# Two transformer layers on one core: the indexer's key group with x stationary, later transfers for the mixed groups, and latents turned in blocks

## The chip, the cores and the metric

The kernel runs on one core of a Trainium2 chip. The metric is the device time of one execution in microseconds, the median of several runs. The core has five engines that run side by side and wait for each other only through semaphores: TensorE (PE in the rows, with its weight loads as PEld), VectorE (DVE), ScalarE (ACT), GpSimd (POOL) and SyncE (SP), which here issues transfers. SP and ACT each have a queue that issues transfers in program order (SPq, ACTq).

## The reference, cut to what matters

Two layers follow one another on x, 256 positions by 2048 channels, all fp32. The parts that the change touches:

```python
# first layer, h = rmsnorm(x)
z = h @ w_in                       # 5200 columns
k_idx = z[..., 5120:5184]          # indexer keys, 64 columns
w_idx = z[..., 5184:5200] * 16 ** -0.5 * 64 ** -0.5
rel = relu(q_idx . k_idx);  iscore = sum over heads of rel * w_idx   # picks 64 keys a query
# second layer, xn = rmsnorm(h)
proj = xn @ w_in_2
c_q, c_kv = proj[..., 3072:3584], proj[..., 3584:3840]   # latents, 512 and 256 columns
qh = rmsnorm(c_q, q_norm) @ w_uq;  kv = rmsnorm(c_kv, kv_norm) @ w_ukv
mixed = g_a * (y_a @ w_branch_a) + g_b * (y_b @ w_branch_b)
h = h + mixed @ w_out
```

## The kernel before, in words

**Products.** All large products are made of three: each operand is split into a high part (rounded to fp32r) and a low part (the rest, also fp32r), and high times high, high times low and low times high are added up. The weights stream in from HBM in chunks, most of them 2 tiles of 128 rows by 512 columns (512 KB). There are 844 chunks in 102 groups; a group is one block of columns of one weight matrix and fills one pair of PSUM banks (`acc`, one bank for each half of 128 positions; two pairs take turns). For a chunk of 512 columns TensorE makes 12 products (`columns`, L754 to L756): a 128 by 128 piece of x is stationary, 512 weight columns move.

**A chunk's way.** A ring of four slots holds the chunks. SP loads one (`load`, L510), ACT copies its high part (`split`, L1081), DVE subtracts for the low part (L1447), TensorE uses it. SP may load chunk c once DVE has split chunk c-4; ACT may split chunk c once TensorE has done chunk c-4; TensorE may start chunk c once DVE has split it.

**Steps.** Everything else is a step: `plan` puts it at a chunk number n by hand (`put(n, ...)`), and each engine runs the steps that are its own. TensorE runs the steps of n after chunk n. ACT and DVE run them after they have split chunk n+3. SP runs them after it has issued the load of chunk n+7 (`at.get(chunk.now - RING - LEAD - 1)`). Nothing is reordered: a step that waits holds back all that stands behind it on its engine or queue.

**Indexer keys** (group 2, chunks 16 and 17, each 8 tiles by 80 columns). `kw_columns` has the weights stationary (128 by 80) and x moving (256 columns): 48 products, L798 to L800, into one bank, with the result turned over (80 rows by 256 positions). ACT copies it to `stage` (`copy_kw`), TensorE turns it back (`turn_kw`, two turns, L745), and DVE scales it into `widx` and `kdup` (`evac_kw`). TensorE then turns `kdup` into the keys (`turn_ki`, step 21), ACT copies them (step 22). The first use is `rel` at step 25.

**Latents.** c_q is group 41 (chunks 378 to 385), c_kv group 42 (386 to 393). ACT evacuates to `stage`, TensorE turns them in the step after (`turn_lat`, 8 and 4 turns, L745), and ACT and DVE split them from the banks one step later (`split_lat`). `w_uq_2` (chunk 418) and `w_ukv_2` (chunk 448) use them.

**Mixed groups.** The gated sum has four blocks of 512 columns, n = 0 to 3. For each there are 4 chunks of `w_branch_a_2` and 4 of `w_branch_b_2`, chunks 516+8n to 523+8n; then comes the output projection `w_out_2` from chunk 548. With b = 524+8n, the chunk number right after the block's last chunk: DVE's step b is `mix_b` (two products with the gate from PSUM, L1699, two sums, L1702, two turns in blocks of 32 by 32, L1601). The blocks are then moved across partitions by 16 transfers of 32 KB each (`move_block`, L382). For n below 3 SP issues four of them in each of the steps b to b+3, and ACT and DVE split the result in step b+7 (`split_mix`, L1239 and L1595). For n = 3 SP issues ten in step b, ACT six in step b+1, and the split is step b+3. The transfers wait for `mix_blocks`, which `mix_b` sets at its end. In the first group of `w_out_2` TensorE waits before its chunk 0 for the split of blocks 0 and 1, before chunks 4 and 5 for the two halves of block 2, and before chunks 6 and 7 for those of block 3:

```python
elif name == "w_out_2" and col == 0:
    need = {k: (mix_low, 8 - n) for k, n in ((0, 4), (4, 3), (5, 2), (6, 1), (7, 0))}
```

Of the kernel before, what the change touches and what calls it, by code (L numbers as in the profile page):

```python
# [54 lines left out]
def plan():  # L55
# [73 lines left out]
    put(b, "copy_kw", len(groups) - 1); put(b + 1, "turn_kw", len(groups) - 1); put(b + 1, "evac_kw")  # L129
    put(b + 3, "turn_ki"); put(b + 4, "copy_ki")  # L130
# [36 lines left out]
    put(b + 1, "turn_lat", "ckv", len(groups) - 1)  # L167
    put(b + 2, "split_lat", "ckv"); put(b + 2, "lat_rstd", "ckv"); put(b + 1, "rope", "kr", len(groups) - 1)
# [65 lines left out]
def two_layer_kernel(nc, a, out):  # L234
# [6 lines left out]
    with ctx:  # L241
# [107 lines left out]
        kw_turned, kw_scaled = sem("kw_turned"), sem("kw_scaled")  # L349
# [15 lines left out]
        p_blocks, p_moved = sem("p_blocks"), sem("p_moved")  # L365
        mix_blocks, mix_moved = sem("mix_blocks"), sem("mix_moved")
# [23 lines left out]

        def shares(part):

            return range(SP_SHARE) if part is None else range(4 * part, 4 * part + 4)
# [6 lines left out]
        def move_mix(queue, n, which):  # L400

            queue.wait_ge(mix_blocks, n + 1)
            move_blocks_of(queue, which, flat_half, flat_stage[1], mix_moved)

# [78 lines left out]
        def _(sp):  # L483
# [12 lines left out]
            def load(name, col, width, c):  # L496
# [233 lines left out]
        def _(pe):  # L730
            chunk, group, splits, copies = Count(), Count(), Count(), Count()
            rels, atts, pvs, lats = Count(), Count(), [0], []
# [58 lines left out]
            def kw_columns(c, g):  # L791
# [60 lines left out]
            def turn_kw(g):  # L852

                wait_bank(0)
                pe.wait_ge(acc_taken[g % 2], 2 * (g // 2 + 1))
                for t in range(NT):
                    last = turn(0, t * KW, stage[0:KW, g % 2, 0, t * P:(t + 1) * P], KW)
                last.then_inc(kw_turned, 1)
                free[0] = (kw_scaled, NT)

            def turn_ki():
                wait_bank(0)
# [115 lines left out]
            def on_turn_stage(g, banks, wait):  # L978
                pe.wait_ge(*wait)
                for b in banks:  # L980
                    wait_bank(b)
                    four(b, lambda cc, t: stage[:, g % 2, t, (2 * b + cc) * P:(2 * b + cc + 1) * P], split_full, 1)
                    splits.now += 1
                    free[b] = (split_lo, splits.now)

            def on_turn_lat(kind, g):
                on_turn_stage(g, range(2 if kind == "cq" else 1), (acc_taken[g % 2], 2 * (g // 2 + 1)))
                lats.append(splits.now)

# [9 lines left out]
            def on_turn_kn(k, g):  # L999
# [6 lines left out]
            mine = {"turn_kw": turn_kw, "turn_ki": turn_ki, "turn_copy": turn_copy, "rel": on_rel, "scores": on_scores,  # L1006
                    "pv": on_pv, "pool_d": on_pool_d, "pool_y": on_pool_y,
                    "turn_lat": on_turn_lat, 
# [26 lines left out]
            while g < len(groups):  # L1035
# [31 lines left out]
        def _(act):  # L1067
# [64 lines left out]

            def on_copy_kw(g):
                finished(g)
                stage_free(g)
                for t in range(NT):
                    act.activation(stage[0:KW, g % 2, 0, t * P:(t + 1) * P], acc[g % 2][0][0:KW, t * P:(t + 1) * P],
                                   ACT.Copy).then_inc(acc_taken[g % 2], 1)
# [92 lines left out]
            def on_split_lat(kind):  # L1231
                o, gain = (cqT, G_CQ) if kind == "cq" else (ckvT, G_CKV)
                for b in range(2 if kind == "cq" else 1):
                    high([o[:, 0, 2 * b], o[:, 0, 2 * b + 1]], b, gain + 2 * b)
# [47 lines left out]
            mine = {"evac": on_evac, "copy_kw": on_copy_kw, "copy_ki": on_copy_ki, "copy2": on_copy2, "copy_k": on_copy_k, "relu": on_relu, "exp": on_exp,  # L1282
# [143 lines left out]
        def _(dve):  # L1426
# [26 lines left out]
            def on_evac_kw():  # L1453

                dve.wait_ge(kw_turned, 1)
                dve.wait_ge(rstd_ready, 1)
                for t in range(NT):
                    r, key = rstd[:, t:t + 1], T[0][:, t * KW:t * KW + IDX_DIM]
                    dve.tensor_scalar(widx[:, t], T[0][:, t * KW + IDX_DIM:(t + 1) * KW], r, 2.0 ** -5, ALU.mult, ALU.mult)
                    dve.tensor_scalar(kdup[:, t, 0:64], key, r, None, ALU.mult)  # L1460
                    dve.tensor_scalar(kdup[:, t, 64:128], key, r, None, ALU.mult).then_inc(kw_scaled, 1)
# [123 lines left out]

            def on_split_lat(kind):
                o, gain = (cqT, G_CQ) if kind == "cq" else (ckvT, G_CKV)
                for b in range(2 if kind == "cq" else 1):
                    low([o[:, 1, 2 * b], o[:, 1, 2 * b + 1]], [o[:, 0, 2 * b], o[:, 0, 2 * b + 1]], b, gain + 2 * b)
# [105 lines left out]
            def on_mix_b(n, g):  # L1695
# [8 lines left out]
                for t in range(NT):  # L1704
# [5 lines left out]
                    "split_pool": on_split_pool, "split_lat": on_split_lat, "split_mix": on_split_mix, "res": on_res,  # L1710
# [208 lines left out]
```

## Time and profile before

| | |
|---|---|
| median of 3 runs | 2373.63 us (2372.42, 2373.67, 2373.63) |
| the profiled execution's own time | 2370.55 us |
| its span, first to last instruction | 2368.8 us |
| mean granted TensorE clock | 0.999 of full speed |
| TensorE busy | 2354.6 us, 99% of the span |
| weight loads busy (beside the products) | 1949.5 us, 82% |
| VectorE, ScalarE, GpSimd busy | 59%, 50%, 3% |
| DMA engines busy with q1 packets | 69.5% |

The page gives busy time by engine, the groups of instructions by line, and the chain of work that ended last. A product's record lasts longer than its place in the stream: the products overlap, so what one costs is the distance from its start to the next one's. In the timeline, a line with "x8" is eight instructions in a row, shown with the first one's start and their whole length; a bracket at the end is idle time before it and what ended it.

### The profile page before, as it was taken

To read this page: it belongs to the slowest core of one execution; us is meant where nothing else is said; L and a number is where in the kernel's file an instruction comes from. 1 tells how busy PE (TensorE), PEld (TensorE's weight loads), DVE (VectorE), ACT (ScalarE), POOL (GpSimd) and SP (SyncE) were. 2 spreads that over 40 slices of the span, in tenths; PEclk is the share of its full clock that TensorE was granted. 3 is DMA by queue.
4 is the path that set the end of the run, shared out by engine and by line. 5 is a ranking of instruction groups with operands and counts; after the bars stand their busy time and mean duration, and the time that the engine had idled before them with its cause. 6 is when DMAs were issued, how large, how long until landed. Compare 5 with 4: busy or idle time off the path is not lost.

```text
span 2368.8 us, 29833 instructions
## 1 busy us (share of the span) xinstructions
PE 2354.6 (99%) x10552; PEld 1949.5 (82%) x10552; DVE 1399.9 (59%) x1586; ACT 1186.1 (50%) x1465; POOL 59.4 (3%) x94
## 2 busy tenths in 40 slices
PE   9999999999999999999999999999999999999998
PEld 7788888888888888888888888878888888888887
DVE  6786465676776765555565554766555555554544
ACT  6445455666666544445455554544544444444443
POOL 0000000000000000001130000000000000000000
PEclk9999999999999999999999999999999999999999
DMA  9776477788787766666787666666777777767664
GB/s 304 195 216 192 153 225 209 215 227 220 202 226 219 206 219 201 201 203 195 210 215 209 181 175 197 200 202 208 230 204 200 209 203 204 209 199 220 194 195 153
DMA packets 490442, 488.24 MB, mean 206 GB/s; under 512 B 248304, under 2 KB 275568, under 8 KB 490224
## 3 DMA queue, kind: packets, MB, share of 16 engines
q1 hardware_dynamic: 467888, 482.85, 69.5%
q10 hardware_dynamic: 22464, 4.20, 0.9%
q8 instruction: 56, 0.92, 0.2%
q14 instruction: 34, 0.28, 0.0%
HBM read 448.12 MB, written 2.10 MB: 190 GB/s over the span
## 4 chain that ended last, share of the span: by engine, by line
PE 96%; SPq 1%; DVE 1%; DMA 1%; ACT 0%; issue 0%; POOLq 0%; POOL 0%; DVEq 0%; ACTq 0%
PE acc L754 31%; PE acc L756 31%; PE acc L755 31%; SPq L382 1%; PE pair_banks L923 1%; DMA w_raw<-in_w_branch_a 1%; DVE w_lo L1447 0%; PE bank L942 0%; ACT w_hi L1081 0%; DMA w_raw<-in_w_in 0%; PE pair_banks L972 0%; PE pair_banks L895 0%; PE acc L780 0%; PE acc L784 0%; PE acc L787 0%
## 5 line engine op out<-in xcount | busy, mean ns | idle before, releaser
L1447 DVE TENSOR_TENSOR w_lo<-w_raw,w_hi 128x1024 fp32r<-128x1024 f32 (+1 forms) x842 | 1024.1, 1220 | 934.8 <-ACT w_hi L1081 933.2
L1081 ACT ACTIVATE w_hi<-w_raw 128x1024 fp32r<-128x1024 f32 (+1 forms) x842 | 886.0, 1055 | 1077.1 <-PE acc L756 980.9
L754 PE MATMUL acc<-w_hi,xT 128*128 128x512 f32 (+1 forms) x2208 | 861.4, 390 | 0.0
L756 PE MATMUL acc<-w_hi,xT 128*128 128x512 f32 (+1 forms) x2208 | 856.8, 388 | 0.0
L755 PE MATMUL acc<-w_lo,xT 128*128 128x512 f32 (+1 forms) x2208 | 856.7, 388 | 0.0
L754 PEld LDWEIGHTS acc<-w_hi,xT 128*128 128x128 f32 x2208 | 414.5, 188 | 87.1 <-issue 2.7
L756 PEld LDWEIGHTS acc<-w_hi,xT 128*128 128x128 f32 x2208 | 414.5, 188 | 85.4
L755 PEld LDWEIGHTS acc<-w_lo,xT 128*128 128x128 f32 x2208 | 414.6, 188 | 83.8
L754 PE MATMUL acc<-w_hi,f_hi 128*128 128x512 f32 x688 | 267.6, 389 | 0.0
L755 PE MATMUL acc<-w_lo,f_hi 128*128 128x512 f32 x688 | 267.6, 389 | 0.0
L756 PE MATMUL acc<-w_hi,f_lo 128*128 128x512 f32 x688 | 267.6, 389 | 0.0
L755 PEld LDWEIGHTS acc<-w_lo,f_hi 128*128 128x128 f32 x688 | 129.2, 188 | 27.0
L754 PEld LDWEIGHTS acc<-w_hi,f_hi 128*128 128x128 f32 x688 | 129.2, 188 | 26.7
L756 PEld LDWEIGHTS acc<-w_hi,f_lo 128*128 128x128 f32 x688 | 129.2, 188 | 26.7
L754 PE MATMUL acc<-w_hi,y_hi 128*128 128x512 f32 x256 | 100.0, 391 | 0.0
L756 PE MATMUL acc<-w_hi,y_lo 128*128 128x512 f32 x256 | 99.6, 389 | 0.0
L755 PE MATMUL acc<-w_lo,y_hi 128*128 128x512 f32 x256 | 99.6, 389 | 0.0
L755 PEld LDWEIGHTS acc<-w_lo,y_hi 128*128 128x128 f32 x256 | 48.1, 188 | 10.0
L754 PEld LDWEIGHTS acc<-w_hi,y_hi 128*128 128x128 f32 x256 | 48.1, 188 | 9.9
L756 PEld LDWEIGHTS acc<-w_hi,y_lo 128*128 128x128 f32 x256 | 48.1, 188 | 9.9
L754 PE MATMUL acc<-w_hi,m_hl 128*128 128x512 f32 x128 | 49.9, 390 | 3.8 <-DVE w_lo L1447 3.8
L755 PE MATMUL acc<-w_lo,m_hl 128*128 128x512 f32 x128 | 49.8, 389 | 0.0
(211 smaller groups left out, 1217.4 us busy)
## 6 DMA issues: line engine op xcount, KB each, us to landing
w_raw<-in_w_up SPq DMA_DIRECT2D x264, 512.0 KB, 4.2
w_raw<-in_w_in SPq DMA_DIRECT2D x198, 512.0 KB, 4.3
w_raw<-in_w_down SPq DMA_DIRECT2D x176, 512.0 KB, 4.5
w_raw<-in_w_gate SPq DMA_DIRECT2D x88, 512.0 KB, 3.7
w_raw<-in_w_out SPq DMA_DIRECT2D x64, 512.0 KB, 4.3
w_raw<-in_w_branch_a SPq DMA_DIRECT2D x16, 512.0 KB, 4.5
w_raw<-in_w_branch_b SPq DMA_DIRECT2D x16, 512.0 KB, 4.4
halves<-stage SPq DMA_DIRECT2D x234, 32.0 KB, 2.7
```

The lines of the kernel that those rows point to most:

```text
L382: return queue.dma_start(dst, src)
L754: pe.matmul(o, l, w_hi[:, slot, k, 0:width], start=start, stop=False)
L755: pe.matmul(o, l, w_lo[:, slot, k, 0:width], start=False, stop=False)
L756: last = pe.matmul(o, m, w_hi[:, slot, k, 0:width], start=False, stop=stop)
L923: last = pe.matmul(pair_banks[:, j, blk * P:blk * P + nk], q[:, blk * P:(blk + 1) * P], k[:, 0:nk], start=alone or blk == 0, stop=alone, s ...
L1081: act.activation(in_slot(w_hi, slot, width), in_slot(w_raw, slot, width), ACT.Copy).then_inc(w_split_hi, 1)
L1447: dve.tensor_tensor(in_slot(w_lo, slot, width), in_slot(w_raw, slot, width), in_slot(w_hi, slot, width).bitcast(F32), ALU.subtract).then_i ...
```

## The change

It has three parts. First, in the group of indexer keys x is stationary (128 by 128) and the 80 weight columns move: 96 products into two banks; `copy_kw` and `turn_kw` are gone, `evac_kw` reads the accumulators one step earlier, and `turn_ki` and `copy_ki` come one step earlier. Second, the transfers of the mixed groups start two steps later: for n below 3 six, six and four in the steps b+2 to b+4, with the split still at b+7; for n = 3 ten from SP and six from ACT, both in step b+2, and the split at b+5. Third, the latents are turned by DVE in blocks of 32 by 32 (`lat_blocks`) and moved across partitions by 16 transfers from SP (four in each of four steps, `move_lat`), and split from SBUF at b+13, in place of the turns on TensorE.

```diff
@@ plan
-    put(b, "copy_kw", len(groups) - 1); put(b + 1, "turn_kw", len(groups) - 1); put(b + 1, "evac_kw")
-    put(b + 3, "turn_ki"); put(b + 4, "copy_ki")
+    put(b, "evac_kw", len(groups) - 1)
+    put(b + 2, "turn_ki", len(groups) - 1); put(b + 3, "copy_ki")
...
-    put(b + 1, "turn_lat", "cq", len(groups) - 1)
-    put(b + 2, "split_lat", "cq"); put(b + 2, "lat_rstd", "cq")
+    put(b + 1, "lat_blocks", "cq", len(groups) - 1)
+    for part in range(4):
+        put(b + 2 + part, "move_lat", "cq", part)
+    put(b + 13, "split_lat", "cq"); put(b + 2, "lat_rstd", "cq")
...
-        for part in range(4) if n < 3 else (None,):
-            put(b + (part or 0), "move_mix", n, part)
+        for part in range(3) if n < 3 else (None,):
+            put(b + 2 + (part or 0), "move_mix", n, part)
         if n == 3:
-            put(b + 1, "move_mix_rest", n)
-        put(b + (7 if n < 3 else 3), "split_mix", n)
+            put(b + 2, "move_mix_rest", n)
+        put(b + (7 if n < 3 else 5), "split_mix", n)
@@ two_layer_kernel
+        def thirds(part):
+
+            return range(SP_SHARE) if part is None else range(6 * part, min(6 * part + 6, 16))
+
+        def latents(kind):
+
+            if kind == "cq":
+                return 0, 4, over_y[0][:], over_y[4][:], cqT, G_CQ
+            return 1, 2, over_y[1][:, 0:CW], over_y[1][:, CW:2 * CW], ckvT, G_CKV
@@ sync
-                            move_mix(sp, args[0], shares(args[1]))
+                            move_mix(sp, args[0], thirds(args[1]))
+            def move_lat(kind, b):
+
+                k, _, blocks_, moved, _, _ = latents(kind)
+                sp.wait_ge(lat_blocks, k + 1)
+                for a_ in range(4):
+                    move_block(sp, moved, blocks_, b, a_).then_inc(lat_moved[k], 16)
@@ tensor, kw_columns
-                    h, l, o = hi[:, k * KW:(k + 1) * KW], lo[:, k * KW:(k + 1) * KW], acc[g][0][0:KW, 0:S]
-                    pe.matmul(o, h, xT_hi[:, kt], start=kt == 0, stop=False)
-                    pe.matmul(o, h, xT_lo[:, kt], start=False, stop=False)
-                    last = pe.matmul(o, l, xT_hi[:, kt], start=False, stop=kt == KT - 1)
+                    h, l = hi[:, k * KW:(k + 1) * KW], lo[:, k * KW:(k + 1) * KW]
+                    for t in range(NT):
+                        o, rows = acc[g][t][:, 0:KW], slice(t * P, (t + 1) * P)
+                        pe.matmul(o, xT_hi[:, kt, rows], h, start=kt == 0, stop=False)
+                        pe.matmul(o, xT_hi[:, kt, rows], l, start=False, stop=False)
+                        last = pe.matmul(o, xT_lo[:, kt, rows], h, start=False, stop=kt == KT - 1)
...
-                    need = {0: (split_lo, lats[0])}
+                    need = {0: (lat_low, 1)}
...
-                    need = {0: (split_lo, lats[1])}
+                    need = {0: (lat_low, 2)}
@@ scalar
             def on_split_lat(kind):
+                k, nq, _, _, o, gain = latents(kind)
+                act.wait_ge(lat_moved[k], 256)
+                for q in range(nq):
+                    last = act.activation(o[:, 0, q].rearrange("p (n k) -> p n k", n=2 * 4), turned_latent(kind, q), ACT.Copy,
+                                          scale=cols[:, gain + q:gain + q + 1])
+                last.then_inc(lat_high, 1)
@@ vector
-            def on_evac_kw():
+            def on_evac_kw(g):
+                finished(g)
...
-                    r, key = rstd[:, t:t + 1], T[0][:, t * KW:t * KW + IDX_DIM]
+                    r, key = rstd[:, t:t + 1], acc[g % 2][t][:, 0:IDX_DIM]
...
+            def on_lat_blocks(kind, g):
+                _, nq, blocks_, _, _, _ = latents(kind)
+                dve.wait_ge(acc_taken[g % 2], 2 * (g // 2 + 1))
+                for t in range(NT):
+                    last = dve.transpose(blocks_.rearrange("p (t b q k) -> p t q b k", t=NT, b=4, q=nq)[:, t],
+                                         stage[:, g % 2, t, 0:nq * P])
+                last.then_inc(lat_blocks, 1)
```

DVE's `split_lat` changes in the same way as ScalarE's: one subtraction for each 128 columns from the moved blocks.

## Rows read from the trace of the kernel before

**Rows 1.** The page: busy times, shares of the last chain, one kind of DMA issue.

```profile
PE 2354.6 (99%) x10552; PEld 1949.5 (82%) x10552; DVE 1399.9 (59%) x1586; ACT 1186.1 (50%) x1465; POOL 59.4 (3%) x94
...
PE 96%; SPq 1%; DVE 1%; DMA 1%; ACT 0%; issue 0%; POOLq 0%; POOL 0%; DVEq 0%; ACTq 0%
...
w_raw<-in_w_in SPq DMA_DIRECT2D x198, 512.0 KB, 4.3
```

**Rows 2.** Waits of TensorE: who waited for whom, us in total, times, longest.

```profile
PE acc L754 <- DVE w_lo L1447: 3.8, 2, 2.5
```

**Rows 3.** Groups by line and shape: busy us, mean ns of one, idle before.

```profile
L1447 DVE TENSOR_TENSOR w_lo<-w_raw,w_hi 128x1024 fp32r<-128x1024 f32 x832 | 1015.8, 1224 | 925.6 <-ACT w_hi L1081 924.0
L1081 ACT ACTIVATE w_hi<-w_raw 128x1024 fp32r<-128x1024 f32 x832 | 878.8, 1059 | 1070.9 <-PE acc L756 974.8 <-DMA w_raw<-in_w_in 36.1 <-DMA w_raw<-in_w_out 20.1
...
L754 PEld LDWEIGHTS acc<-w_hi,xT 128*128 128x128 f32 x2208 | 414.5, 188 | 87.1 <-issue 2.7
...
L798 PEld LDWEIGHTS acc<-xT,w_hi 128*80 128x80 f32 x16 | 2.4, 148 | 0.0
```

**Rows 4.** Timeline around the group of indexer keys: start us, us, engine, line.

```profile
49.27 0.39 PE L755 MATMUL acc<-w_lo,xT 128*128 128x512 f32 x1
...
50.17 0.39 PE L756 MATMUL acc<-w_hi,xT 128*128 128x512 f32 x1
...
50.40 0.28 PE L798 MATMUL acc<-xT,w_hi 128*80 128x256 f32 x1
50.40 0.15 PEld L799 LDWEIGHTS acc<-xT,w_hi 128*80 128x80 f32 x1
...
55.87 0.28 PE L800 MATMUL acc<-xT,w_lo 128*80 128x256 f32 x1
```

**Rows 5.** The same view: the first scores, on plain fp32 operands.

```profile
143.17 1.47 PE L923 MATMUL pair_banks<-k1T,q1T 128*128 128x128 f32 x8
...
144.71 0.40 PE L755 MATMUL acc<-w_lo,xT 128*128 128x512 f32 x1
```

**Rows 6.** The same view: turns on TensorE, of keys and of the first latents.

```profile
61.47 0.30 PE L745 MATMUL bank<-ident,stage 80*128 80x80 f32 x2
...
61.88 0.40 PE L755 MATMUL acc<-w_lo,xT 128*128 128x512 f32 x1
...
1092.84 1.04 PE L745 MATMUL bank<-ident,stage 128*128 128x128 f32 x8
...
1093.86 0.31 PE L755 MATMUL acc<-w_lo,xT 128*128 128x320 f32 x1
```

**Rows 7.** The same view: the sync queue's transfers in the mixing stage.

```profile
1545.54 3.49 SPq L382 DMA_DIRECT2D halves<-stage  x4
...
1562.80 6.38 SPq L382 DMA_DIRECT2D halves<-stage  x10
```

**Rows 8.** The same view: VectorE at the first mixed group and the last.

```profile
1491.55 1.30 DVE L1601 STREAM_TRANSPOSE stage<-stage 128x512 f32<-128x512 f32 x2
...
1558.82 1.28 DVE L1699 TENSOR_TENSOR gate<-acc,gate 128x512 f32<-128x512 f32 x2
...
1561.46 1.30 DVE L1601 STREAM_TRANSPOSE stage<-stage 128x512 f32<-128x512 f32 x2
1562.69 1.18 DVE L1447 TENSOR_TENSOR w_lo<-w_raw,w_hi 128x1024 fp32r<-128x1024 f32 x1
...
1570.91 1.43 DVE L1595 TENSOR_TENSOR m_hl<-halves,m_hl 128x256 fp32r<-128x256 f32 x4 [0.42 <-ACT m_hl L1239]
```

**Rows 9.** The same view: ScalarE's queue and copies at the last mixed group.

```profile
1562.80 4.13 ACTq L382 DMA_DIRECT2D halves<-stage  x6
...
1570.46 1.34 ACT L1239 ACTIVATE m_hl<-halves 128x256 fp32r<-128x256 f32 x4 [1.42 <-DMA halves<-stage]
```

**Rows 10.** The same view: TensorE's idle starts in the output projection.

```profile
1564.02 0.47 PE L754 MATMUL acc<-w_hi,m_hl 128*128 128x512 f32 x1 [1.29 <-DVE w_lo L1447]
...
1569.50 0.47 PE L754 MATMUL acc<-w_hi,m_hl 128*128 128x512 f32 x1 [2.48 <-DVE w_lo L1447]
```

More of the change, by code:

```diff
@@ L162, in plan @@
     put(b, "evac", "stage", len(groups) - 1); put(b + 1, "lat_square", "cq", len(groups) - 1)
-    put(b + 1, "turn_lat", "cq", len(groups) - 1)
-    put(b + 2, "split_lat", "cq"); put(b + 2, "lat_rstd", "cq")
+    put(b + 1, "lat_blocks", "cq", len(groups) - 1)
+    for part in range(4):
+        put(b + 2 + part, "move_lat", "cq", part)
+    put(b + 13, "split_lat", "cq"); put(b + 2, "lat_rstd", "cq")
     b = group("w_in_2", 3584, 320, whole, "x")
     put(b, "evac", "ckv", len(groups) - 1); put(b + 1, "lat_square", "ckv", len(groups) - 1)
-    put(b + 1, "turn_lat", "ckv", len(groups) - 1)
-    put(b + 2, "split_lat", "ckv"); put(b + 2, "lat_rstd", "ckv"); put(b + 1, "rope", "kr", len(groups) - 1)
+    put(b + 1, "lat_blocks", "ckv", len(groups) - 1)
+    for part in range(4):
+        put(b + 2 + part, "move_lat", "ckv", part)
+    put(b + 13, "split_lat", "ckv"); put(b + 2, "lat_rstd", "ckv"); put(b + 1, "rope", "kr", len(groups) - 1)
     put(b + 4, "turn_kr"); put(b + 5, "copy_kr")
@@ L365, in two_layer_kernel @@
         p_blocks, p_moved = sem("p_blocks"), sem("p_moved")
+        lat_blocks, lat_high, lat_low = sem("lat_blocks"), sem("lat_high"), sem("lat_low")
+        lat_moved = [sem("cq_moved"), sem("ckv_moved")]
         mix_blocks, mix_moved = sem("mix_blocks"), sem("mix_moved")
@@ L403, in move_mix, with turned_latent @@
             move_blocks_of(queue, which, flat_half, flat_stage[1], mix_moved)
+        def latents(kind):
+            if kind == "cq":
+                return 0, 4, over_y[0][:], over_y[4][:], cqT, G_CQ
+            return 1, 2, over_y[1][:, 0:CW], over_y[1][:, CW:2 * CW], ckvT, G_CKV
+        def turned_latent(kind, q):
+            _, nq, _, moved, _, _ = latents(kind)
+            return moved.rearrange("p (n q k) -> p n q k", n=2 * 4, q=nq)[:, :, q]
         def p_source(which, pair):
@@ L849, in stream, with turn_ki @@
                 group.now += 1
-            def turn_kw(g):
+            def turn_ki(g):
                 wait_bank(0)
                 pe.wait_ge(acc_taken[g % 2], 2 * (g // 2 + 1))
[L856 to L862, printed above, removed]
                 turn(0, 0, kdup[:, 0])
@@ L976, in on_pool_y @@
                     free[2 + w] = (split_lo, splits.now)
[L978 to L988, printed above, removed]
             def on_turn_kr():
@@ L1004, in on_turn_kn @@
                 free[0] = (copy_done, copies.now)
-            mine = {"turn_kw": turn_kw, "turn_ki": turn_ki, "turn_copy": turn_copy, "rel": on_rel, "scores": on_scores,
+            mine = {"turn_ki": turn_ki, "turn_copy": turn_copy, "rel": on_rel, "scores": on_scores,
                     "pv": on_pv, "pool_d": on_pool_d, "pool_y": on_pool_y,
-                    "turn_lat": on_turn_lat,
                     "turn_kr": on_turn_kr, "turn_kn": on_turn_kn}
@@ L1131, in copied @@
                 act.activation(out_, T[bank][:, 0:width], ACT.Copy, scale=scale).then_inc(copy_done, 1)
[L1133 to L1138, printed above, removed]
             def on_copy_ki():
@@ L1231, in on_split_lat @@
             def on_split_lat(kind):
-                o, gain = (cqT, G_CQ) if kind == "cq" else (ckvT, G_CKV)
-                for b in range(2 if kind == "cq" else 1):
-                    high([o[:, 0, 2 * b], o[:, 0, 2 * b + 1]], b, gain + 2 * b)
+                k, nq, _, _, o, gain = latents(kind)
[4 more added lines that the diff above has]
+                last.then_inc(lat_high, 1)
             def on_split_mix(n):
@@ L1451, in finished @@
                 dve.wait_ge(w_used, first[g] + len(groups[g][3]))
-            def on_evac_kw():
-                dve.wait_ge(kw_turned, 1)
+            def on_evac_kw(g):
+                finished(g)
                 dve.wait_ge(rstd_ready, 1)
                 for t in range(NT):
-                    r, key = rstd[:, t:t + 1], T[0][:, t * KW:t * KW + IDX_DIM]
-                    dve.tensor_scalar(widx[:, t], T[0][:, t * KW + IDX_DIM:(t + 1) * KW], r, 2.0 ** -5, ALU.mult, ALU.mult)
+                    r, key = rstd[:, t:t + 1], acc[g % 2][t][:, 0:IDX_DIM]
+                    dve.tensor_scalar(widx[:, t], acc[g % 2][t][:, IDX_DIM:KW], r, 2.0 ** -5, ALU.mult, ALU.mult)
                     dve.tensor_scalar(kdup[:, t, 0:64], key, r, None, ALU.mult)
-                    dve.tensor_scalar(kdup[:, t, 64:128], key, r, None, ALU.mult).then_inc(kw_scaled, 1)
+                    dve.tensor_scalar(kdup[:, t, 64:128], key, r, None, ALU.mult).then_inc(acc_taken[g % 2], 1)
             def on_headsq(name, g):
@@ L1584, in on_split_pool @@
                     low([y_lo[:, k], y_lo[:, k + 1]], [y_hi[:, k], y_hi[:, k + 1]], 2 + w, G_POOL + k)
-            def on_split_lat(kind):
-                o, gain = (cqT, G_CQ) if kind == "cq" else (ckvT, G_CKV)
-                for b in range(2 if kind == "cq" else 1):
-                    low([o[:, 1, 2 * b], o[:, 1, 2 * b + 1]], [o[:, 0, 2 * b], o[:, 0, 2 * b + 1]], b, gain + 2 * b)
+            def on_lat_blocks(kind, g):
[5 more added lines that the diff above has]
+                last.then_inc(lat_blocks, 1)
+            def on_split_lat(kind):
+                k, nq, _, _, o, gain = latents(kind)
+                dve.wait_ge(lat_high, k + 1)
+                for q in range(nq):
+                    lo_, hi_ = (o[:, n, q].rearrange("p (n k) -> p n k", n=2 * 4) for n in (1, 0))
+                    last = dve.scalar_tensor_tensor(lo_, turned_latent(kind, q), cols[:, gain + q:gain + q + 1],
+                                                    hi_.bitcast(F32), ALU.mult, ALU.subtract)
+                last.then_inc(lat_low, 1)
             def on_split_mix(n):
```

9 lines of the change are left out of this document (5 added, 4 removed).

## The prediction

> **What bounds the kernel now.** The page comes first: TensorE is busy 99% of the span, and 96% of the chain that ended last is its products [rows 1]. A microsecond taken from TensorE's stream, or added to it, is a microsecond of the kernel; work on the other engines counts only where it makes TensorE wait. The waits of TensorE say where it does so in mid-kernel: twice, for the low parts of weights [rows 2]. The timeline puts both into the output projection of layer two, before chunks 552 and 553 [rows 10]. The idle shown there is 1.29 and 2.48 us; the real loss is more, as each record before it reaches 0.39 - 0.23 = 0.16 us past its place and the first product after it is 0.08 longer: 1.53 and 2.72, together 4.25 us. Five products of 512 columns take 50.40 - 49.27 = 1.13 us, 0.227 each [rows 4], so a chunk of twelve is 2.72 us; 512 columns at the 2.4 GHz level are 0.213 of the 0.227, and 13 ns are left over per change of weights.
>
> **Part 1, the indexer's keys.** Before: 48 products from 50.40 to 55.87 [rows 4], 47 distances of 0.116 us, so 5.6 us in all; 256 columns are 107 ns of it, 10 ns are left over. After: 96 products of 80 columns, 33 ns of streaming each. So short a product no longer hides its weight load. A load of 128 columns is on record for 188 ns, one of 80 for 148 [rows 3]: 40 ns for 48 columns, 0.83 ns a column, hence 107 ns of loading for 128 columns, the rest being a fixed part. A load starts with the product before it (both at 50.40 [rows 4]) and must be through before its own product starts, so the distance is at least 107 ns, and with the 10 or so left over 0.116: 96 x 0.116 = 11.1 us, a term of +5.5. That x's high part is stationary twice in a row saves nothing by the profile, since L754 and L755 share theirs in the same way and every product has its own load. Bounds: if streaming set the distance (33 + 13 ns), 96 x 0.047 = 4.5 us, -1.1. If so narrow a product ran at the rate of plain fp32, it would be slower: the first scores are 8 instructions, 4 of 128 and 4 of 256 columns, and TensorE is free for L754 0.23 before L755, at 144.48, so 1536 columns in 1.31 us [rows 5], two clocks a column; a plain product is two such instructions, four clocks. Then 0.133 + 0.013 = 0.147 each, 14.1 us, +8.5. I take 11.1, because the slope of the loads is of this very operand type and the other two ends need something that no row shows.
>
> The Trainium skill has a rule that speaks for the low end: by "TensorE: Matmul & The Clock Gate", section on Fast Weight Load, weights of 128 columns that are not fp32 load about twice as fast. By it the part would cost 96 x (53 + 13) ns = 6.4 us, +0.8. The trace disagrees so far: 128 columns, at 188 ns, lie on the slope from the 80-column load and not below it [rows 3].
>
> The turns that go: two of 80 columns, from 61.47 to 61.65 (L755 at 61.88 less 0.23), 0.2 us at most; eight of the first latents, from 1092.84 to 1093.71 (1093.86 less the 0.15 of a 320-column product), 0.87 us, 0.109 each [rows 6]; four more for the second, 0.44. Together -1.5. The scaling on DVE one step earlier costs nothing on the path: it waits for chunk 17, done before it can split chunk 21, and its result is wanted by TensorE two chunks on and by the first use at step 25. ScalarE loses two small copies.
>
> **Part 2, latents in blocks.** DVE gets four block turns (0.65 us each at 512 columns [rows 8], so at most 2.6), SP gets 32 transfers. One costs SP 0.638 us (ten in 6.38 [rows 7]); four and a load of some 0.6 are 3.2 us per chunk against 2.72, so SP falls behind by about 2 us in four chunks, twice. That is covered: SP may load chunk c when chunk c-4 is split, and that split begins when chunk c-8 is done, so 7 chunks less the 2.3 us of the split, 16.7 us, before TensorE needs c; landing (4.3 from issue [rows 1]), high part and low part want 6.6 of them. The split at b+13 has its transfers landed long before, and the first user is chunk 418, eleven after the last split. I take 0; with the cover gone it would be up to 2.
>
> **Part 3, the mixed groups.** This part decides the sign. Let E be the end of DVE's two turns for block n; E is 1491.55 + 1.30 = 1492.85 for n = 0 and 1562.76 for n = 3 [rows 8], so blocks follow at 23.3 us, where eight chunks are 21.8: engines fall behind by 1.5 us a block, and this lag is what shows up as the idle before chunk 552. With the change, from E: two low parts (1.23 each, the line's mean [rows 3]) E + 2.4; load of b+9 0.6, E + 3.0; six transfers 3.84, load, six, load, four (16 x 0.638 and two loads at 0.64 in all), last issued E + 14.5; landed 1.3 later (1569.18 to the copy at 1570.46 [rows 7, 9]), E + 15.8; ScalarE, which reached this step earlier and waits, four copies 1.3, then its next high part 1.06 [rows 3], low part 1.23, and 3.94 of mixing and turning (1558.82 to 1562.76): the next E is at + 23.4. That is no better than before, though transfers no longer wait for DVE; SP still has to issue 16 and ScalarE now stands at the split. Before, though, SP also paused in some transfers (four in 3.49 rather than 2.55 [rows 7]); if pauses recur, up to 2 us come on top. So the last E comes 0.3 to 2.3 later, I take 1.1.
>
> For n = 3 the end is what counts. TensorE wants the first half of block 3 before chunk 554. Before: chunk 552 starts at E + 1.3, 553 at E + 6.7 (held up because ScalarE was busy with its six transfers, 4.13 us [rows 9], before it could split 553), 554 at E + 9.5; block 3 was split by then (1570.91 + 0.7 = E + 8.9 [rows 8]). After: ScalarE splits 553 first, so 553 starts at E + 4.0 and 554 could at E + 6.7. But SP's step 550 stands behind the load of chunk 557, that behind the low part of 553, E + 2.4; load 0.6, ten transfers 6.4, landing 1.3, first copies and low parts 1.2: E + 11.9. A wait of 5.2 us before chunk 554 takes the place of the 2.72 before 553: + 2.4. With the later E, **+3.5**. Bounds: even with everything landed at once, the split at step 553 stands behind the split of chunk 556, which wants chunk 552 done: 1.06 + 1.23 + 0.7 = 3.0 after chunk 553 starts, 0.3 past its 2.72; so at best 4.25 - 0.3 = 3.9 us are gained. At worst 2.3 + 2.4 and a pause in the ten transfers of 1: +5.7.
>
> **Sum.** 5.5 - 1.5 + 3.5 = +7.5 us. On the profiled execution's own 2370.55 that is 2378.1; this one was 3.1 below the median of 2373.63, so the median should be 2381.1, 0.32% up. A measurement can tell some 0.2% from no change, 4.7 us.
>
> **Rivals.**
> A. The forecast, new wait before chunk 554 and products bound by loads, with its own spread of 2378 to 2384: 0.57.
> B. Not slower: the later transfers do what they could do. The place is chunks 552 to 554; the price is -3.9 for +3.5. It decides if the split of block 3 is through within 3 us of chunk 553's start, that is, if SP's ten transfers land before E + 7 or so. Then 5.5 - 1.5 - 3.9 = +0.1, 2373.7. For it: ScalarE's and SP's transfers no longer stand before the splits of 552 and 553. Against: ten transfers alone are 6.4 us and cannot begin before E + 3. 0.10.
> C. In between: old waits gone, the new one no longer than they were. +4.0, 2377.7. 0.13.
> D. Narrow products bound by something less than a 107 ns load (the fast load, or streaming): -1.1 to +0.8 for 5.5, so with part 3 as forecast +0.9 to +2.8, 2375.5; with B as well -6.5 to -4.6, about 2368. 0.05 and 0.02.
> E. Four clocks a column: +8.5 for 5.5, 2384.1; with the worst of part 3 2386.3. 0.13.
>
> B, C and the first of D lie within 0.2%, the second of D is faster, A and E are slower save for the lower edge of A (0.05). Faster 0.02, within 0.33, slower 0.65. The range leaves out the second of D, the lower half of B, and the top of E: 2373.5 to 2386.
>
> **What would show it.** Part 1: the new products of 80 columns start 0.11 to 0.12 apart and take 11 us from first to last; 0.15 would be E, 0.07 or less D. The 12 turns of latents are gone, with no new idle in front of w_uq_2. Part 3: TensorE's waits name the low part of block 3 (m_hl, L1595 before) as what releases it before chunk 554, for about 5 us; SP's ten transfers start some 3 us after the last turns, not at once; ScalarE waits for a landing before the copies to m_hl in every block. The forecast is wrong if the output projection shows no idle at chunk 554, or if the key group takes less than 8 us.

## The result, and the profile after

The changed kernel takes 2389.93 us (median of 4, 2389.26 to 2391.07), the kernel before in the same session 2373.31 (median of 4): 1.0076 times as long, 95% interval 1.0063 to 1.0088. It is slower by more than was forecast: +16.6 us by the medians for +7.5, and outside the range. The profiled executions are further apart, 2389.74 and 2370.55, because the one of before lay 2.8 us under its median; by the spans it is 2388.0 - 2368.8 = 19.2, and the stages below add up to that.

The page after, beside [rows 1]:

```profile
PE 2369.5 (99%) x10586; PEld 1962.4 (82%) x10586; DVE 1402.2 (59%) x1590; ACT 1185.9 (50%) x1463; POOL 59.1 (2%) x94
...
PE 95%; DMA 1%; DVE 1%; SPq 1%; ACT 0%; issue 0%; ACTq 0%; POOLq 0%; POOL 0%; DVEq 0%
```

TensorE is the bound as before, and is busy for 14.9 us longer with 34 more instructions. Its idle time grew by only some 4. So most of the loss is inside busy time, where no view of waits shows it. The waits of TensorE after, beside [rows 2]:

```profile
PE acc L783 <- DVE m_hl L1614: 4.0, 1, 4.0
PE acc L783 <- DVE w_lo L1454: 3.7, 3, 2.0
...
PE bank L965 <- DMA halves<-over_y: 1.0, 1, 1.0
```

The first is the wait that was forecast (the low part of block 3, before chunk 554), the second is three waits for low parts of weights, the third is new in the middle of layer two.

To place the 19.2 us, I took from each trace the time at which the last product before a chunk ends, and subtracted those of before. The differences by stage, in us, for the full change and for the three kernels with one part of it each (described below):

| stage | after | keys alone | mixing alone | latents alone | forecast |
|---|---|---|---|---|---|
| start-up, to chunk 16 | +0.2 | +0.2 | +0.6 | +0.7 | 0 |
| keys and the two chunks behind, 16 to 20 | +11.6 | +11.6 | 0 | 0 | +5.5 |
| the keys' turns, 20 to 34 | -0.2 | -0.2 | 0 | 0 | -0.2 |
| the latents' turns, 378 to 402 | -1.35 | 0 | 0 | -1.35 | -1.3 |
| 402 to 448 | +1.3 | +0.4 | 0 | 0 | 0 |
| mixing, 544 to 555 | +7.6 | -1.5 | +8.0 | +1.7 | +3.5 |
| all, to chunk 844 | +19.1 | +10.5 | +8.6 | +1.1 | +7.5 |

No part of the change touches the start-up, so its +0.2 to +0.7 are differences from one execution to another. Two terms missed, the keys by 6 and the mixing stage by 4. For the keys, TensorE by windows (length, then busy us and instructions of PE, PEld, DVE, ACT, POOL; granted clock; DMA share; GB/s), first the stretch from the first narrow product on:

```profile
50.00:56.00 6.00, 6.00 (x54) 5.88 (x52) 1.66 (x2) 2.21 (x3) 0.00 (x0) 1.00 0.95 285
56.00:64.00 8.00, 8.00 (x44) 8.00 (x43) 2.44 (x3) 1.06 (x1) 0.00 (x0) 0.56 0.77 173
64.00:72.00 8.00, 8.00 (x26) 6.55 (x26) 2.46 (x8) 2.12 (x2) 0.00 (x0) 0.59 0.44 99
```

TensorE is busy for every one of these 22 us, yet the granted clock falls from 1.00 to 0.56. The timeline of the same stretch shows where:

```profile
50.58 0.20 PE L829 MATMUL acc<-w_hi,xT 128*128 128x80 f32 x1
...
56.53 0.28 PE L829 MATMUL acc<-w_hi,xT 128*128 128x80 f32 x1
56.64 0.28 PE L830 MATMUL acc<-w_lo,xT 128*128 128x80 f32 x1
56.75 0.29 PE L831 MATMUL acc<-w_hi,xT 128*128 128x80 f32 x1
56.86 0.39 PE L829 MATMUL acc<-w_hi,xT 128*128 128x80 f32 x1
57.06 0.42 PE L830 MATMUL acc<-w_lo,xT 128*128 128x80 f32 x1
57.27 0.41 PE L831 MATMUL acc<-w_hi,xT 128*128 128x80 f32 x1
...
64.95 0.41 PE L831 MATMUL acc<-w_hi,xT 128*128 128x80 f32 x1
...
69.58 0.63 PE L784 MATMUL acc<-w_lo,xT 128*128 128x512 f32 x1
70.00 0.63 PE L785 MATMUL acc<-w_hi,xT 128*128 128x512 f32 x1
70.43 0.48 PE L783 MATMUL acc<-w_hi,xT 128*128 128x512 f32 x1
...
71.22 0.40 PE L783 MATMUL acc<-w_hi,xT 128*128 128x512 f32 x1
71.45 0.39 PE L784 MATMUL acc<-w_lo,xT 128*128 128x512 f32 x1
```

The narrow products start 0.11 apart, then from 56.86 on 0.21 apart; the first products of 512 columns behind them start 0.43 apart, and from about 70.7 on 0.23 to 0.24. That is the 1.2 GHz level for nearly 14 us, and TensorE was busy without a gap for over 6 us before it. From the first narrow product to the last (64.95) the group takes 14.4 us, where the prediction's sign was 11. The mixing stage after, four timelines in turn (TensorE, the sync queue, ScalarE with its queue, VectorE; a bracket is idle time and its releaser), beside [rows 7 to 10]:

```profile
1554.02 0.47 PE L783 MATMUL acc<-w_hi,y_hi 128*128 128x512 f32 x1 [1.49 <-DVE w_lo L1454]
...
1578.63 0.47 PE L783 MATMUL acc<-w_hi,m_hl 128*128 128x512 f32 x1 [2.03 <-DVE w_lo L1454]
...
1579.52 0.63 PE L783 MATMUL acc<-w_hi,m_hl 128*128 128x512 f32 x1
1579.95 0.63 PE L784 MATMUL acc<-w_lo,m_hl 128*128 128x512 f32 x1
...
1589.95 0.80 PE L783 MATMUL acc<-w_hi,m_hl 128*128 128x512 f32 x1 [4.02 <-DVE m_hl L1614]
1590.54 0.63 PE L784 MATMUL acc<-w_lo,m_hl 128*128 128x512 f32 x1
```

```profile
1516.33 2.50 SPq L387 DMA_DIRECT2D halves<-stage  x4
...
1573.54 6.48 SPq L530 DMA_DIRECT2D w_raw<-in_w_out  x3
1580.06 6.63 SPq L387 DMA_DIRECT2D halves<-stage  x10
1586.73 1.61 SPq L530 DMA_DIRECT2D w_raw<-in_w_out  x3
```

```profile
1521.57 1.34 ACT L1246 ACTIVATE m_hl<-halves 128x256 fp32r<-128x256 f32 x4 [3.24 <-DMA halves<-stage]
...
1577.41 3.88 ACTq L387 DMA_DIRECT2D halves<-stage  x6
1581.39 2.97 ACT L1092 ACTIVATE w_hi<-w_raw 128x1024 fp32r<-128x1024 f32 x3 [7.05 <-issue]
1588.69 1.33 ACT L1246 ACTIVATE m_hl<-halves 128x256 fp32r<-128x256 f32 x4 [4.33 <-DMA halves<-stage]
```

```profile
1503.11 1.30 DVE L1620 STREAM_TRANSPOSE stage<-stage 128x512 f32<-128x512 f32 x2
...
1576.07 1.30 DVE L1620 STREAM_TRANSPOSE stage<-stage 128x512 f32<-128x512 f32 x2
...
1589.13 1.43 DVE L1614 TENSOR_TENSOR m_hl<-halves,m_hl 128x256 fp32r<-128x256 f32 x4 [3.15 <-ACT m_hl L1246]
```

The order is the forecast's. E, the end of the last block's turns, is 1577.37 (the first lines of the sync queue and of ScalarE belong to block 0, whose E is 1504.41). SP's ten transfers start 2.7 later, ScalarE stands 4.33 us for their landing, and TensorE starts chunk 554 at E + 12.6. Two things were not forecast: the wait before chunk 544 (1554.02), and half the clock twice, in chunk 552 (products 0.43 apart) and again from 1590.54 on.

### The profile page after: what moved, and what is told of

It reads as the page before. It is cut to its first block, busy times and chain, and to the rows that moved or that the text cites. A ratio compares the mean times of both kernels' runs of the same rounds, so it can differ in the third digit from the quotient of the medians.

```text
span 2388.0 us, 29932 instructions
## 1 busy us (share of the span) xinstructions
PE 2369.5 (99%) x10586; PEld 1962.4 (82%) x10586; DVE 1402.2 (59%) x1590; ACT 1185.9 (50%) x1463; POOL 59.1 (2%) x94
## 4 chain that ended last, share of the span: by engine, by line
PE 95%; DMA 1%; DVE 1%; SPq 1%; ACT 0%; issue 0%; ACTq 0%; POOLq 0%; POOL 0%; DVEq 0%
PE acc L783 30%; PE acc L785 30%; PE acc L784 30%; SPq L387 1%; PE pair_banks L946 1%; DVE w_lo L1454 1%; DMA halves<-stage 0%; PE bank L965 0%; PE acc L809 0%; PE acc L813 0%; PE acc L816 0%; PE pair_banks L995 0%; ACT w_hi L1092 0%; DMA w_raw<-in_w_branch_a 0%; PE pair_banks L918 0%
## 5 line engine op out<-in xcount | busy, mean ns | idle before, releaser
L783 PE MATMUL acc<-w_hi,m_hl 128*128 128x512 f32 x128 | 51.5, 402 | 6.3 <-DVE m_hl L1614 4.0
L785 PE MATMUL acc<-w_hi,m_hl 128*128 128x512 f32 x128 | 50.9, 398 | 0.0
```

The costliest lines, as they stand in the source:

```text
L783: pe.matmul(o, l, w_hi[:, slot, k, 0:width], start=start, stop=False)
L785: last = pe.matmul(o, m, w_hi[:, slot, k, 0:width], start=False, stop=stop)
```

## The experiments

Each kernel was compared with the kernel before on the same chip. The first four share one session (before: 2371.04, 22 runs), the last four another (before: 2371.66, 33 runs).

**Keys alone.** Only part 1 of the change; mixed groups and latents as before.

```diff
 # kernel after
-    put(b + 1, "lat_blocks", "cq", len(groups) - 1)
...
+    put(b + 1, "turn_lat", "cq", len(groups) - 1)
...
-        for part in range(3) if n < 3 else (None,):
-            put(b + 2 + (part or 0), "move_mix", n, part)
+        for part in range(4) if n < 3 else (None,):
+            put(b + (part or 0), "move_mix", n, part)
...
```

> The kernel before with part 1 alone (keys with x stationary). Theory K, clock: the 96 products start 0.113 us apart (10.9 us, +5.3 over the 5.6 of before), and some us into them TensorE's granted clock falls from full to half, in which loads and products take twice as long (0.213 apart), until some us after the group: 11.5 to 12 us slower in all, 2385. Rival: products bound by their loads alone, the fall of the clock in the changed kernel was chance: 5 us slower, 2378.5, no half clock behind the start of the kernel.

Measured: 2381.10 us (5 runs), ratio 1.0041 (1.0027 to 1.0055), +10.1 by the medians. By stages the key group costs what it costs in the full change, +11.6, as expected with the fall of the clock, and the turns give back 0.2. Before the mixing stage it is 12.0 behind, after it 10.5: of the two stalls of before [rows 10] the first is gone here, although nothing in that stage was edited. So how engines stand to each other when they enter the stage is worth a microsecond or two, and no sum of terms sees that.

**Keys with 240 columns moving.** Part 1 again, with the same loads and the same number of products, but each streams 240 columns. The sums in the 160 extra columns are read by nobody, and those in the first 80 are unchanged.

```diff
 # kernel of part 1 alone, kw_columns
-                hi, lo = in_slot(w_hi, slot, KW), in_slot(w_lo, slot, KW)
+                hi, lo = (ring[:, slot].rearrange("p k n -> p (k n)") for ring in (w_hi, w_lo))
...
-                    h, l = hi[:, k * KW:(k + 1) * KW], lo[:, k * KW:(k + 1) * KW]
+                    h, l = hi[:, k * KW:(k + 3) * KW], lo[:, k * KW:(k + 3) * KW]
...
-                        o, rows = acc[g][t][:, 0:KW], slice(t * P, (t + 1) * P)
+                        o, rows = acc[g][t][:, 0:3 * KW], slice(t * P, (t + 1) * P)
```

> Part 1 alone, but each product streams 240 columns, 80 real ones and the 160 that lie behind them in the slot, whose results nobody reads: same number of loads and products. If loads of 107 ns set the distance and the clock fell because the array had little to stream, the distance stays near 0.115 and the clock stays full: 96 x 0.115 = 11.0, 5.4 us slower than before, 2378.7, so 6 us faster than the narrow products that do a third of the work. If the clock falls for another reason (many loads, short instructions): 2385 as with the narrow ones. If streaming set the distance all along: 240 columns take 0.1 + 0.013, no verdict from the distance, only from the clock.

Measured: 2375.29 us (10 runs), ratio 1.0016 (1.0006 to 1.0025), +4.3 by the medians. Three times the streaming is 5.8 us faster than 80 columns. The windows of the same 16 us, first of keys alone, then with 240 columns, and three of the wide products:

```profile
56.00:72.00 16.00, 16.00 (x68) 14.87 (x68) 4.83 (x11) 3.18 (x3) 0.00 (x0) 0.58 0.59 137
```

```profile
56.00:72.00 16.00, 16.00 (x98) 14.13 (x97) 8.38 (x13) 5.57 (x6) 0.00 (x0) 1.00 0.67 150
```

```profile
58.35 0.28 PE L826 MATMUL acc<-w_lo,xT 128*128 128x240 f32 x1
58.47 0.28 PE L827 MATMUL acc<-w_hi,xT 128*128 128x240 f32 x1
58.58 0.27 PE L825 MATMUL acc<-w_hi,xT 128*128 128x240 f32 x1
```

Busy 16.00 of 16.00 in both, but the clock is 0.58 in one and 1.00 in the other. As long as the clock is full, the products are 0.11 to 0.12 apart whether 80 or 240 columns move (0.112 on average in both traces). This splits the term of the keys. From chunk 16 to 20 it is +5.1 with 240 columns and +11.6 with 80: the distance at the full clock costs 5.1, and the clock 6.5 on top. Idle time did not lower the clock, and with the same loads the wider products kept it. That is what this pair shows; it gives no rule for other widths.

**Latents alone.** Only part 2; the rest as before.

```diff
 # kernel after
-    put(b, "evac_kw", len(groups) - 1)
-    put(b + 2, "turn_ki", len(groups) - 1); put(b + 3, "copy_ki")
+    put(b, "copy_kw", len(groups) - 1); put(b + 1, "turn_kw", len(groups) - 1); put(b + 1, "evac_kw")
+    put(b + 3, "turn_ki"); put(b + 4, "copy_ki")
...
```

> The kernel before with part 2 alone (latents in blocks). Theory: the turns' 1.36 us are gained and nothing is lost: 1.4 us faster, 2372. Rival: the 32 added transfers bring the wait of 1.3 us before the products with P at chunk 442 that the changed kernel shows: 0 to 0.1, 2373.3, that wait in the trace again.

Measured: 2371.00 us (10 runs), ratio 0.9999 (0.9989 to 1.0008): no difference, neither the 1.4 us faster of the theory nor the wait of the rival. Its trace, one execution, shows the gain and a loss. The turns' 1.35 us go at chunks 386 to 402, and no wait comes in their place. In the mixing stage +1.7 come back: the two stalls are much those of before (1.41 and 2.47 idle), but behind the second one the clock drops, which it did not in the trace of before. The windows of the same stretch, latents alone and before:

```profile
1565.00:1578.00 13.00, 10.53 (x40) 8.27 (x39) 8.01 (x10) 7.47 (x10) 0.00 (x0) 0.87 0.66 200
```

```profile
1565.00:1578.00 13.00, 10.52 (x47) 8.39 (x46) 8.20 (x10) 7.48 (x10) 0.00 (x0) 1.00 0.64 198
```

The same 10.5 us busy hold 40 products for 47. So a stall of 2.5 us can be followed by half the clock or not; the traces do not show what decides. It need not be the kernel: of the 55 executions of before in the two sessions, 19 had a mean granted clock of 0.998 and took 2372.4 us on average, the other 36 had 0.999 or more and took 2371.0. The trace of before has 0.999 and no half clock in the stage, so its stages may stand for the faster executions only, and where the 1.35 us went in the median of latents alone stays open.

**Mixing alone.** Only part 3; keys and latents as before.

```diff
 # kernel before
-        for part in range(4) if n < 3 else (None,):
-            put(b + (part or 0), "move_mix", n, part)
+        for part in range(3) if n < 3 else (None,):
+            put(b + 2 + (part or 0), "move_mix", n, part)
         if n == 3:
-            put(b + 1, "move_mix_rest", n)
-        put(b + (7 if n < 3 else 3), "split_mix", n)
+            put(b + 2, "move_mix_rest", n)
+        put(b + (7 if n < 3 else 5), "split_mix", n)
```

> The kernel before with part 3 alone (mixed groups' transfers two steps later). Theory M: the long wait for block 3 before chunk 554 and the half clock after it do not need parts 1 and 2: 7.5 us slower (6 to 8), 2381, with 9 us of idle and 2 to 3 of half clock in the chunks 547 to 556. Rival: the step is right but its size came with the shifted phase of the other parts: 3 to 4 us slower, 2377, no half clock.

Measured: 2378.93 us (6 runs), ratio 1.0030 (1.0017 to 1.0042), +7.9. TensorE waits 5.6 us for the low part of block 3 and 3.6 for low parts of weights, and the stage costs +8.0, as expected with half the clock behind the long wait (granted 0.62 from 1578 to 1585). The turns end at 1493.4 for block 0 and 1566.0 for block 3, 24.2 us a block, against 23.3 before and 23.4 forecast. The loss is the same as in the full change and does not need the other parts. Its halves were then tried one at a time.

**Last block alone (n = 3) and first three alone.** The transfers and the split of block 3 two steps later with blocks 0 to 2 as before, and the other way about.

```diff
 # kernel before, last block alone
-            put(b + (part or 0), "move_mix", n, part)
+            put(b + (part or 0) + (2 if n == 3 else 0), "move_mix", n, part)
         if n == 3:
-            put(b + 1, "move_mix_rest", n)
-        put(b + (7 if n < 3 else 3), "split_mix", n)
+            put(b + 2, "move_mix_rest", n)
+        put(b + (7 if n < 3 else 5), "split_mix", n)
```

```diff
 # kernel of part 3 alone, first three alone
-            put(b + 2 + (part or 0), "move_mix", n, part)
+            put(b + (2 if n < 3 else 0) + (part or 0), "move_mix", n, part)
         if n == 3:
-            put(b + 2, "move_mix_rest", n)
-        put(b + (7 if n < 3 else 5), "split_mix", n)
+            put(b + 1, "move_mix_rest", n)
+        put(b + (7 if n < 3 else 3), "split_mix", n)
```

> The kernel before with only block 3 changed: its ten and six transfers in step b+2 and its split at b+5; blocks 0 to 2 as before. Theory L: the last block's late transfers carry most of part 3. Idle before chunk 554 of 5 to 6 us in place of the 2.7 before 553, then about 2 us of half clock: 4 to 6 us slower, 2376. Rival: the new order of blocks 0 to 2 carries it: under 2 us slower here, 2372.5.

> The kernel before with only blocks 0 to 2 changed (six, six and four transfers in steps b+2 to b+4), block 3 as before. Theory L: the lag of a block is no smaller than before, idle of 1.8 us appears before chunk 547 or 548 and the one before 552 stays: 1.5 to 3 us slower, 2373.5. Rival: this part does what it was for, since transfers no longer wait for DVE: 1.5 us faster, 2369.5.

Measured: last block alone 2375.07 (10 runs), ratio 1.0015 (1.0006 to 1.0025), +3.4; first three alone 2374.80 (10 runs), ratio 1.0011 (1.0002 to 1.0021), +3.1. Together +6.5, against +7.9 for part 3 as a whole, within the intervals. The expectations were 4 to 6 and 1.5 to 3, so by the medians the last block came out too low and the first three just above; in their mixing stages the traces have +4.2 and +4.5. TensorE's start of chunk 554 with the last block alone:

```profile
1574.32 0.80 PE L754 MATMUL acc<-w_hi,m_hl 128*128 128x512 f32 x1 [5.42 <-DVE m_hl L1595]
```

SP's ten transfers start here at 1564.60, 2.7 us after the turns' end at 1561.92. Until chunk 554 this kernel is 3.6 us ahead of before, since both old stalls have shrunk to 0.7 us in all; then it loses 7.8 at one chunk, 5.4 of them the wait and 2.2 the half clock behind it (granted 0.60 from 1574 to 1580). That is rival B and the forecast in one trace: the gain was real, and what replaced it larger. The first three alone show the lag and no wait for block 3:

```profile
1543.30 0.47 PE L780 MATMUL acc<-w_hi,y_hi 128*128 128x512 f32 x1 [1.54 <-DVE w_lo L1474]
...
1567.70 0.47 PE L780 MATMUL acc<-w_hi,m_hl 128*128 128x512 f32 x1 [2.05 <-DVE w_lo L1474]
...
1573.16 0.47 PE L780 MATMUL acc<-w_hi,m_hl 128*128 128x512 f32 x1 [2.48 <-DVE w_lo L1474]
```

A third stall of 1.54 us has joined the two of before. It stands before chunk 544, the first of the last branch group; my expectation put it a few chunks later. Behind the last of the three, of 2.48, the clock is low (granted 0.66 from 1573 to 1578), which makes 1.6 of the stage's 4.5.

**Transfers shared out between the queues.** If SP's issue time is what makes the blocks late, ScalarE should take some of it where it waits anyway. For n below 3, SP issues three and ScalarE one transfer in each of four steps (SP b+1 to b+4, ScalarE b+2 to b+5); for n = 3 eight each, SP at once, ScalarE after the split of chunk 553. So shares and steps change together here, and no run takes them apart.

```diff
 # kernel before
-            put(b + (part or 0), "move_mix", n, part)
-        if n == 3:
-            put(b + 1, "move_mix_rest", n)
+            put(b + (1 + part if n < 3 else 0), "move_mix", n, part)
+            put(b + 2 + (part or 0), "move_mix_rest", n, part)
...
-                            move_mix(sp, args[0], shares(args[1]))
+                            move_mix(sp, args[0], range(8) if args[1] is None else range(4 * args[1], 4 * args[1] + 3))
...
-            def on_move_mix_rest(n):
-                move_mix(act, n, range(SP_SHARE, 16))
+            def on_move_mix_rest(n, part):
+                move_mix(act, n, range(8, 16) if part is None else range(4 * part + 3, 4 * part + 4))
```

> The kernel before with the transfers of the mixed groups shared out anew: for blocks 0 to 2 SP issues three in each of the steps b+1 to b+4 and ACT one in each of b+2 to b+5, split at b+7; for block 3 SP issues eight in step b, ACT eight in step b+2, split at b+3. Theory: SP stays under 2.72 us a chunk (0.6 + 3 x 0.64 = 2.5), so no lag is carried from block to block, E comes 6.3 us after chunk 547's end, and neither 552, 553 nor 554 waits: the 4.25 us of idle go, 4 us faster, 2367. Rival: ScalarE's share delays its splits so that the idle only changes place: within 1 us of before, 2371.

Measured: 2367.51 us (11 runs), ratio 0.9985 (0.9976 to 0.9994): 4.2 us faster than before by the medians, as expected. Blocks follow at 22.8 us, and one wait is left in the stage:

```profile
PE acc L753 <- DVE m_hl L1594: 1.7, 1, 1.7
```

The traced execution, 2369.17, is one of the slowest of the eleven; in its mixing stage it is 4.2 us ahead of before until chunk 554 and, after this wait, 2.25. All 22 executions of this kernel and the next have a mean granted clock of 0.999 or more.

**The same with the latents in blocks.** Part 2 of the change on top.

```diff
 # kernel of latents alone; the mixing stage as in the edit above
         for part in range(4) if n < 3 else (None,):
-            put(b + (part or 0), "move_mix", n, part)
-        if n == 3:
-            put(b + 1, "move_mix_rest", n)
+            put(b + (1 + part if n < 3 else 0), "move_mix", n, part)
+            put(b + 2 + (part or 0), "move_mix_rest", n, part)
...
```

> The same with the latents in blocks besides. Theory: both gains add, 4.2 + 1.4 = 5.6 us faster than before, 2365.4, with no half clock behind the start of the kernel. Rival: what the latents' part gains is lost again later, as when it stood alone: no faster than with the shared transfers alone.

Measured: 2366.63 us (11 runs), ratio 0.9979 (0.9970 to 0.9988), 5.0 faster for 5.6 expected and the lowest median of all. Its page:

```profile
PE 2353.4 (100%) x10540; PEld 1948.8 (82%) x10540; DVE 1401.1 (59%) x1590; ACT 1185.3 (50%) x1465; POOL 60.2 (3%) x94
```

There is no idle left in the mixing stage, and the granted clock is 1.00 from 14 to 2355 us. By stages the latents' turns give -1.35 and the mixing stage -3.95, close to the -4.25 that the two stalls of before were worth. Against the kernel before it with shared transfers it is only 0.9 faster by the medians, within their spread; whether the latents' gain adds up is not shown.

## Why the prediction was wrong

**Part 1: the distance was right, the clock was not.** The step that failed is the one that makes of the keys "96 x 0.116 = 11.1 us, a term of +5.5". The distance measured at the full clock is 0.112 for the 0.116 of the sum; neither streaming (0.047) nor four clocks a column (0.147) sets it. It fits the load of 128 columns, and a least distance for every product is out, since the two turns of 80 columns in before start 0.07 apart (0.30 us for two, each record 0.23 [rows 6]); but no run loads fewer columns under so narrow a product. With the clock held full, 240 columns wide, the term is +5.1. What the sum left out is that these 96 products did not keep the clock. It took the full clock of before for granted in a stretch unlike any in before, and its list of signs to look for did not name it either. 6.5 us, measured with 80 and with 240 columns, is what that cost. It is the largest piece of the miss. The turns of the keys gave 0.2, as forecast.

By the rule on Fast Weight Load of the Trainium skill ("TensorE: Matmul & The Clock Gate") the estimate for the distance was 0.066; the trace says 0.112. So the low end of the term, and with it rival D, is out. The same page's section on HAM oscillation puts a mid-kernel fall of the clock down to gaps in TensorE's work while it waits for data. The mixing stage fits that in part: the clock is low there behind stalls of 2.0 and 4.0 us in the full change and behind one of 2.5 in latents alone, but not behind stalls of 2.5 in before and in keys alone. The keys do not fit, as their records leave no gap.

**Part 2: right as a stage.** The twelve turns gave 1.35 us (1.3 forecast), no wait came in front of `w_uq_2`, and SP's falling behind was covered. The median of latents alone does not show the gain.

**402 to 448: not foreseen.** 1.3 us go in a wait of TensorE before `pv`, in the step after chunk 442. The timelines of TensorE, of the sync queue and of ScalarE's queue:

```profile
1253.86 0.67 PE L965 MATMUL bank<-halves,va 128*128 128x256 f32 x2 [1.04 <-DMA halves<-over_y]
```

```profile
1239.99 2.53 SPq L439 DMA_DIRECT2D halves<-over_y  x4
...
1243.21 4.24 SPq L439 DMA_DIRECT2D halves<-over_y  x4
```

```profile
1242.06 4.09 ACTq L439 DMA_DIRECT2D halves<-over_y  x4
```

Four such transfers take SP 2.53 us a moment earlier and 4.24 here; ScalarE's queue pauses in the same microseconds, and one packet of the instruction queue (q8) falls between 1243 and 1247. No part of the change touches these lines. Such pauses come all through the kernel, and a kernel that is 10 us later meets them at other instructions; latents alone and mixing alone lose nothing in this stage, keys alone loses 0.4 us. The pauses and the packets go together: of the 107 issues other than weight chunks that took over 1.15 us in all ten traces (their first 20 us left out), 100 overlap a q8 packet, and of the 11,695 that took 0.8 or less, 102 do. That the packet causes the pause was not tested.

**Part 3: the mechanism was right, its size was not.** +7.6 for +3.5, in three pieces. The first two share a term that was sized too small: "landed 1.3 later", the time from the last issue of a block to ScalarE's copy.
- The lag. "the next E is at + 23.4" was too short: 1503.11 to 1576.07 is three blocks, 24.3 each. The last E is 3.05 later than in before, once the 11.56 that the stage starts late are taken off, for the 1.1 that I took and the 2.3 that I held for the worst. Issuing was as forecast: block 0's last transfer is issued at 1518.83, E + 14.4 (14.5). But the copy starts at 1521.57, 2.7 us later and not 1.3, and it is 2.3 and 2.2 later in blocks 1 and 2. One pause of 0.9 in the transfers of block 2 comes on top. The lag shows as the stall before chunk 544. First three alone confirms that this half comes from blocks 0 to 2.
- The last block. Chunk 554 starts at E + 12.6 for a forecast E + 11.9, and E + 9.5 in before: +3.0 for +2.4. The transfers were as forecast, E + 2.7 for the ten (E + 3), 6.6 for issuing them (6.4); the landing was not, 2.0 from the last issue (1586.69) to the copy (1588.69) for 1.3. The wait itself reads 4.0 us and not the 5.2 of the forecast only because chunk 552 ran at half the clock and used up part of it; in mixing alone it is 5.6.
- The clock. The stall is followed by products 0.43 apart. In chunk 554, which takes 4.2 us for 2.7, that adds 1.5 (7.6 less the 3.05 and the 3.0). It was no term.

**The rivals.** A was the mechanism of part 3, too cheap, and its spread ended at 2384. B and C are out for the change as made: the ten transfers landed at about E + 11.3 and not before E + 7, and the stage's stalls came to 7.5 us of idle for 3.8 in before. But B's argument held for the place: with the transfers shared over both queues and SP's eight of block 3 left at once, the stage gained 2.25 us in one trace and 3.95 in the other, of the 4.25. D and E are out by the distance of 0.112. That the key group took 14.4 us, close to E's 14.1, is chance: its distance was 0.112 and then 0.213, never 0.147.

**Sum.** +5.1 for the distance of the keys' products, +6.5 for their clock, -0.2 and -1.35 for turns, +1.3 for the pause, +7.6 for the mixing stage, +0.2 at the start: 19.2, as the spans say. The single parts as medians, +10.1, 0.0 and +7.9, make 18.0 against 16.6 for all of them: they add up within their intervals.

## What to carry to other kernels

Before a product is made narrower, price it by its weight load, and then ask what the granted clock will do: the group of short products here cost twice, in distance and in the clock, and the clock stayed low for the wide products that followed. The later transfers did not gain here, because the queue that issued them made them late; count issue time, per queue, from the last instruction ahead of the transfers, take the time to land from a row of the same kind of block, and share transfers with a queue that has time to spare. A stall can cost more than its idle time, through the clock behind it, and a stage that lives on small slacks can move by a microsecond or two when anything earlier moves.

## What the runs showed of the hardware that was not expected

- The granted clock halved with TensorE's records busy for 16.00 of 16.00 us: products of 80 columns with a load of 128 each gave 0.58, 240 columns with the same loads 1.00. The wider kernel was 5.8 us faster (2375.29 against 2381.10).
- For fp32r operands, products of 80 and of 240 columns behind loads of 128 columns have the same distance at the full clock, 0.112 us on average.
- Behind stalls of TensorE of 2.46 to 2.48 us the clock was low in three traces (granted 0.76 from 1568 to 1575 in latents alone, 0.66 from 1573 to 1578 with 240 columns and in first three alone) and full in two (before and keys alone). Behind the stall of 1.7 with shared transfers it was full.
- Single transfers that a queue otherwise issues in 0.6 us take it up to 2.3 now and then; at 1244 us of the changed kernel it was so in both queues at once (2.3 and 2.0). 100 of the 107 issues of over 1.15 us overlap a packet of the instruction queue.
